# Two hybrid layers on one core: spectra and convolutions of the Hyena mixer in one stage, RWKV preparation in another order, output projection by pairs of tiles, first expert loaded during routing

## The reference

```python
def hier_moe(h, wg, bg, we, be, w_gate, w_up, w_down):      # 4 groups x 8 experts, top 2 in the best group
    ...
    hg = lax.ragged_dot(xs, w_gate, sizes); hu = lax.ragged_dot(xs, w_up, sizes)
    ys = lax.ragged_dot(jax.nn.silu(hg) * hu, w_down, sizes)
def hyena_mixer(u, ...):                                     # u: 1024 x 1536, three parts v, x1, x2
    h = hyena_filters(L, ...)                                # a small network's output @ w4, times a window
    z = x1 * long_conv(v, h[:, 0, 0], h[:, 0, 1], sk[0])     # both directions, by spectra of length 2048
    z = x2 * long_conv(z, h[:, 1, 0], h[:, 1, 1], sk[1])
def rwkv_mixer(u, ...):                                      # 8 heads of 64
    d = w0 + einsum('dblr,drc->dblc', tanh(wd), w2); decay = exp(-exp(-0.5) * sigmoid(d))
    a = sigmoid(a0 + einsum('dblr,drc->dblc', ad, a2)); g = sigmoid(gd) @ g2
    kk = heads(k * k_k); kk = kk / maximum(sqrt(sum(kk * kk, -1)), 1e-12)
    ...                                                      # the scan over tokens, both directions
    y = (y - mu_y) * rsqrt(var_y + RW_GN_EPS) * gn_w + gn_b  # per head
    y = (y + bonus) * g
def hybrid_layer(x, ...):
    x = layer_norm(DN_ALPHA * x + (g_h * y_h + g_r * y_r) @ w_o)
    ffn = (silu(x @ ffn_w_gate) * (x @ ffn_w_up)) @ ffn_w_down
    return layer_norm(DN_ALPHA * x + ffn)
```

## Time and profile before

| | |
|---|---|
| median of 3 runs | 4329.37 us (4329.35 to 4332.1) |
| profiled execution | 4336.35 us |
| its span | 4334.6 us |
| busy in it | PE 85%, DVE 66%, ACT 38%, POOL 1% |
| mean granted TensorE clock | 0.919 of full |
| bytes moved by DMA | 707.47 MB, mean 163 GB/s |

### The profile page before, as it was taken

The page is one execution under the profiler, slowest core; times in us unless marked ns, Lnnn a source line. Parts: engine busy times, 40 slices in busy tenths (PEclk is TensorE's granted clock), DMA queues, the critical chain, the costliest instruction groups (busy, mean ns, idle before and its releaser), DMA issues. The chain is left out here.

```text
span 4334.6 us, 62648 instructions
## 1 busy us (share of the span) xinstructions
PE 3668.8 (85%) x24897; PEld 2941.5 (68%) x24897; DVE 2840.1 (66%) x3459; ACT 1630.3 (38%) x2142; POOL 56.7 (1%) x50
## 2 busy tenths in 40 slices
PE   6999987979759999919999676439998786999897
PEld 4888876868747777717888232129996565888786
DVE  4775327966458888968875778765555547666455
ACT  3322114545247777733332110433332223333244
POOL 0000000000010000010000000000000000000000
PEclk8999999989779999959999788669999898999999
DMA  5933217545389999852332231471110432222455
GB/s 207 334 136 109 92 60 231 177 146 196 136 327 399 398 398 398 320 185 88 117 117 78 101 149 61 121 178 42 42 42 9 170 107 78 88 78 78 175 190 170
DMA packets 358292, 707.47 MB, mean 163 GB/s; under 512 B 55912, under 2 KB 160376, under 8 KB 355866
## 3 DMA queue, kind: packets, MB, share of 16 engines
q1 hardware_dynamic: 322698, 578.90, 38.7%
q10 hardware_dynamic: 20528, 67.11, 4.1%
q0 software_dynamic: 14816, 57.95, 3.7%
HBM read 536.18 MB, written 179.25 MB: 165 GB/s over the span
## 5 line engine op out<-in xcount | busy, mean ns | idle before, releaser
L1767 DVE TENSOR_TENSOR moe_wg_lo<-moe_wg,moe_wg_hi 128x2048 fp32r<-128x2048 f32 x68 | 155.7, 2292 | 68.9 <-ACT moe_wg_hi L1721 68.8
L156 PE MATMUL g_ps<-h1T_hi,g_w_lo 128*128 128x512 f32 x448 | 176.0, 393 | 6.9 <-DVE g_w_lo L355 6.9
L157 PE MATMUL g_ps<-h1T_lo,g_w_hi 128*128 128x512 f32 x448 | 175.5, 392 | 0.0
L158 PE MATMUL g_ps<-h1T_hi,g_w_hi 128*128 128x512 f32 x448 | 175.3, 391 | 0.0
L1721 ACT ACTIVATE moe_wg_hi<-moe_wg 128x2048 fp32r<-128x2048 f32 x68 | 130.3, 1920 | 95.5 <-DMA moe_wg<-in_exp_w_gate 95.5
L3929 DVE TENSOR_TENSOR x3T_lo<-fd_w_raw,x3T_hi 128x1024 fp32r<-128x1024 f32 x66 | 80.8, 1224 | 123.3 <-ACT x3T_hi L3858 123.1
L156 PE MATMUL g_ps<-x2T_hi,g_w_lo 128*128 128x512 f32 x352 | 140.0, 398 | 24.6 <-DVE g_w_lo L582 24.6
L2743 PE MATMUL rs_p_p<-rs_pm,rs_qx 64*64 64x64 f32 x2048 | 157.3, 217 | 0.0
L156 PE MATMUL fd_acc<-x3T_hi,x3T_lo 128*128 128x512 f32 x352 | 139.3, 396 | 20.0 <-DVE x3T_lo L3932 20.0
L1767 DVE TENSOR_TENSOR moe_wu_lo<-moe_wu,moe_wu_hi 128x2048 fp32r<-128x2048 f32 x68 | 152.6, 2285 | 2.3 <-ACT moe_wu_hi L1721 2.3
L156 PE MATMUL g_ps<-g_w_hi,h1T_lo 128*128 128x512 f32 x384 | 149.6, 390 | 0.0
(11 more groups left out here) (679 smaller groups left out, 10678.9 us busy)
## 6 DMA issues: line engine op xcount, KB each, us to landing
moe_wg<-in_exp_w_gate SPq DMA_DIRECT2D x68, 1024.0 KB
moe_wu<-in_exp_w_up SPq DMA_DIRECT2D x68, 1024.0 KB
moe_wd<-in_exp_w_down SPq DMA_DIRECT2D x66, 1024.0 KB
fd_w_raw<-in_ffn_w_down SPq DMA_DIRECT2D x66, 512.0 KB, 4.3
go_w_raw<-in_w_out SPq DMA_DIRECT2D x64, 512.0 KB
g_w<-in_w_in SPq DMA_DIRECT2D x52, 512.0 KB, 5.8
g_w<-in_w_in SPq DMA_DIRECT2D x22, 1024.0 KB
moe_x<-s_xs SPq DMA_DIRECT2D x34, 512.0 KB
```

The costliest lines, as they stand in the source:

```text
L156: pe.matmul(out, l[1], r[0], start=(k == 0), stop=False)
L157: pe.matmul(out, l[0], r[1], start=False, stop=False)
L158: return pe.matmul(out, l[0], r[0], start=False, stop=(k == kt - 1))
L1767: v.tensor_tensor(lo[:, q * m:q * m + m], w[:, q * m:q * m + m], hi[:, q * m:q * m + m], ALU.subtract).then_inc(sem_lo, 1)
```

## The change

Five pieces, in the order of the program:

1. **Routing** issues the loads of expert 0's three weight matrices (6.29 MB) behind its own loads, into raw buffers that now live outside both stages; `tile_exp` gets N_LIST more columns: whether a tile is used and has another expert than the tile before. **The expert loop** loads weights where that column says so, by two more register loads per tile; expert 0's loads are left out by the same condition.
2. **The two Hyena stages become one** (`hy`). The window is loaded before the transform table, v at the stage's start. PE turns v before the last transform and x1 after it, ACT alone copies both; DVE goes on from the last spectrum spread to the convolution's. The inverse table, x1 and the first spectrum planes are loaded during n = 3, into buffers that came free.
3. **RWKV preparation**: the low-rank inputs and weights are loaded first and decay, rate and gate of block 0 computed first; then the key's statistics, held as 128 x 256 (four column blocks at 32 rows each) instead of 32 x 1024, and spread through a zeroed 128 x 1024 tile (`spread_rows`). **RWKV finish** uses the constants that preparation left in its tiles, and the same 128 x 256 form.
4. **Output projection**: row tiles in the order 0, 4, 1, 5, 2, 6, 3, 7; the differences after each pair; the last sums as a group of three pairs (128 x 1536) and one of the last pair (128 x 512). It also loads the feed-forward's first gate weights (1 MB) during its norms.
5. **Feed-forward**: group 0 is there already, and its first unit is split before the four sums.

```diff
@@ route
+            for dst, src in first:
+                sp.dma_start(dst[:, :, :], rows(src)).then_inc(w_in, 16)
+            sp.wait_ge(w_in, past(16 * len(first)))
...
+            v.tensor_scalar(te[:, N_LIST + 1:N_LIST + 2], te[:, 0:1], 0.0, None, ALU.not_equal)
+            v.tensor_tensor(te[:, N_LIST + 2:], te[:, 1:N_LIST], te[:, 0:N_LIST - 1], ALU.not_equal)
+            v.tensor_copy(tile_exp[:, N_LIST:N_LIST + 1], te[:, N_LIST:N_LIST + 1])
+            v.drain()
+            v.tensor_scalar(tile_exp[:, N_LIST + 1:], te[:, N_LIST + 1:], te[:, N_LIST:N_LIST + 1], None, ALU.mult)
@@ experts
-                             cond=(n_used > j)).then_inc(sem[q], 16)
+                             cond=(limit > j)).then_inc(sem[q], 16)
...
-                e, e1 = expert(j), expert(j + 1)
+                e, e1, new, new1 = expert(j), expert(j + 1), fresh(j), fresh(j + 1)
@@ hyena, SP
-            sp.dma_start(tb[:, :, :], table).then_inc(table_in, 16)
             sp.dma_start(win[:, :, :], window).then_inc(win_in, 16)
-            for n in range(4):
+            sp.dma_start(tb[:, :, :], f_table).then_inc(table_in, 16)
+            sp.dma_start(raw[:, :, :], rows(conv[0:HY_W, :])).then_inc(v_in, 16)
...
+            for n in range(NF4):
+                if n == NF4 - 1:
+                    sp.wait_ge(turned, past(NT))
+                    sp.dma_start(raw[:, :, :], rows(conv[HY_W:2 * HY_W, :])).then_inc(x_in, 16)
+                    sp.wait_ge(windowed, past(16))
+                    sp.dma_start(it, i_table).then_inc(i_in, 16)
+                    sp.wait_ge(filt, past(16))
+                    for b in range(2):
+                        sp.wait_ge(spec_out[b], past(16 * (9 - b)))
+                    for i in range(NS):
+                        planes_in(0, i)
@@ hyena, PE
+                else:
+                    pe.wait_ge(v_in, past(16))
+                    pe.wait_ge(windowed, past(16))
+                    turn(z_act)
                 transform(n)
...
+            turn(x_act)
+            pe.wait_ge(taken, past(N_OUT))
+            pe.wait_ge(x_act, past(NT))
@@ rw_prepare and rw_finish
+def spread_rows(v, ri, riz):
+    for g in range(4):
+        r = slice(32 * g, 32 * g + 32)
+        e = v.tensor_copy(riz[r, g * RQ:g * RQ + RQ], ri[r, :])
...
+                        for g in range(4):
+                            mm = pe.matmul(p_r[:, 0:RQ], sel_s[:, q, 96 - 32 * g:224 - 32 * g], sq[:, q % 2, g * RQ:g * RQ + RQ],
+                                           start=(q == 0 and g == 0), stop=(q == RP - 1 and g == 3))
@@ product_norm
-                sp.dma_start(r[:, t % 2], x[t * P:t * P + P, :]).then_inc(x_in[t % 2], 16)
+                sp.dma_start(r[:, t % 2], x[ORDER[t] * P:ORDER[t] * P + P, :]).then_inc(x_in[t % 2], 16)
...
+            sp.dma_start(*early).then_inc(early_in, 16)
...
-                if t >= NT // 2:
-                    mix(t - NT // 2)
+                if t % 2:
+                    mix(t // 2)
...
+            low_sums(0, NP - 1, left_high, left_low)
+            low_sums(NP - 1, NP, mixed_high, mixed_low)
@@ ffn_up
-        w = [raw[:, 2 * b:2 * b + 2].rearrange("p a (k c) -> p (a k) c", c=256) for b in range(2)]
+        w = [w_first, raw[:, 2:4].rearrange("p a (k c) -> p (a k) c", c=256)]
...
+            split(0, 0)
             add_sums(0)
-            for i in range(7):
+            for i in range(1, 7):
                 split(0, i)
```

552 lines of the change are left out of this document (287 added, 265 removed).

## The result

| | before | after |
|---|---|---|
| median | 4329.56 us (4 runs, 4329.35 to 4332.1) | 4283.68 us (4 runs, 4277.1 to 4286.99) |
| profiled execution, its span | 4336.35, 4334.6 us | 4286.99, 4285.2 us |
| ratio | | 0.9892, 95% interval 0.9879 to 0.9904 |

The forecast was 4277 with a range of 4260 to 4296. The profiled executions differ by 49.4 us, the medians by 45.9. The times of the changed kernel scatter over 10 us, those of before over 3.

What follows compares the result with a forecast made beforehand. PE and DMA were taken to bound the expert loop, head-of-stage waits the other four places; 5 + 23 + 2 + 4 + 8.5 + 9.6 = 52 us off 4336.35 gave 4284, or 4277 for the median; range 4260 to 4296.

Steps and rivals of the forecast that it cites:

- Experts: Route and expert loop: preloading the first expert's weights brings its first products 5 us sooner; −5 us (0 to −10).
- the argument from bytes: Expert loop: 4.2 MB still to come at 1239.7, 10.5 us at 398 GB/s, is the most DMA can give.
- Hyena: Joint Hyena stage: −23 us (−18 to −27) from the join, −2 (0 to −4) from loading the window first.
- The slip: Hyena: 6.1 MB of loads ahead of the last eight spectrum stores delay the last transform's end from 2533.9 to near 2539.4.
- The window's order: Hyena's start: window loaded before the transform table, so the four window products are packed closer; −2 us (0 to −4).
- rw_prepare: RWKV preparation: reciprocal falls from 6.54 to 1.65 us, statistics move behind decay, rate and gate; −4 us (+4 to −6.5).
- The rival of the lower clock: PE stays at 1.2 GHz in the new stages: rw_prepare +8, rw_finish +2.5, hyena +3; 4291 us, chance 0.08.
- rw_finish: RWKV finish: no wait for constants, first matmuls at the upper clock, shorter reciprocal chain; −8.5 us (−6.5 to −11).
- Projection and feed-forward: Pairs end the projection's low sums sooner, first gate weights already loaded, first unit split first; −9.6 us (−8 to −11).
- Half of the join: Rival, Hyena: stores behind loads and ACT's copies hold PE back; −11 in place of −23, 4289 us, chance 0.11.
- the whole head start for the experts: Rival, expert loop: the weight stream, 10.5 us earlier, sets the end; 4271 us, chance 0.08.
- SP as a bound: Rival, expert loop: extra register loads and conditions make SP the bound, slower from 12.7 us per expert; chance 0.03.

Runs made afterwards that it cites:

- hy_late: Changed kernel, with the four spectrum planes, top plane and inverse table loaded behind the last eight spectrum stores: median 4280.65 us, Hyena stage 329.6 us.
- hy_only: Kernel before, with only its two Hyena stages replaced by the joint one: median 4309.74 us, ratio to before 0.9953.
- no_early: Changed kernel, with the feed-forward's first gate weights loaded at that stage's start again: median 4289.28 us, ratio to before 0.9904.

## Why the prediction was right, point by point

The forecast was 6.7 us below the measured median, well inside its range; the sum of 52 us stands against 45.9 by the medians.

- **Experts, −5 of 0 to −10: −6.5, in the mean of the profiles −5.5.** The size was right, the steps to it only in part. ACT's four halves without a gap came as forecast. The first load of expert 1 came 0.3 us sooner by the clock of the span, not 1.8 to 2.2; in the stage's own time the other nine profiles with the preload show 1.9 to 2.1 us, as forecast, but the stage opens 1.0 to 1.2 us later in all ten, where I had put 0.45 (the routing's first scatter is 0.43 us late, the rest is unexplained). Silu of the first expert, 1248.44, was 1.6 us sooner, not 5, and the last expert's silu stands 5.0 us nearer to the first's. The gain fits the argument from bytes: 6.3 MB less have to pass within the loop, and PE, whose own pace is 17.7 us and not 18.0 per expert, catches up in five to ten experts; then the weights bound it again. That the 5 us hit was luck in part: I had taken it from products that come 4 to 5 us sooner, and they came 1.6 us sooner.
- **Hyena, −25 of −18 to −31: −23.0, over nine profiles −23 to −30.** DVE's spread for the convolution stands 135.1 us after the stage's first load in place of 165.1, 30.0 sooner: 26.6 by the join, 1.1 by the first spread, and 2.3 by the transforms between, where PE had less of the lower clock (the first full one took 15.70 us in place of 17.00); 9.3 of it are lost again before PE's first inverse product (34.5 us behind the spread in place of 25.2), which leaves 20.7, in the forecast's 20 to 22.5; and 2.3 come behind it, 1.8 of them by the upper clock (3.60 us for what took 5.37). The slip was named rightly, as hy_late shows, and was larger where the lower clock came on top. The window's order: DVE's first product came 3.0 us sooner in the stage (+14.8 in place of +17.8), but the spread behind it only 1.1 us, since the filter matmuls are in its way; over all profiles with the new order that spread stands at +22.1 to +24.1, before at +23.3, so this part (−2) gave 1 us or nothing.
- **What was misread in the Hyena term.** The second input load of before landed 14.1 us after its issue, but the table was issued behind it, not ahead, so these are two loads of 2.1 MB in 14.5 us, some 290 GB/s, and not 398; the seven loads took 18.8 us in place of my 15.4. And the figures of this term are measured against one profile of before that was probably 7 us long in just these stages: by hy_only's median the join gives 20.6 us, 4 less than the forecast and within its range.
- **rw_prepare, −4 of +4 to −6.5: −0.1, over six profiles +0.8 to −3.8, −1.1 in the mean.** This is the term that was mis-sized. I put kk at 33 to 37 us after the first load; it came at 34.6 to 38.8. The failed step is "four squares with their matmuls to 2779 to 2780.6": in the stage's own time that was +28, and it was +30.6 (PE to 2753.77). From the root to the last copy 3.8 us passed, where I had 1.5 to 3.5, and the spread took 3.8 us, my upper value. In no_early, where the granted clock was 1.00 through the statistics, the same step ended at +28.1, as forecast, and the stage was 143.1 us, 3.8 below before: the chain was counted rightly for the upper clock, and the clock was the part put too low. The rival of the lower clock thus happened here by half (+3.9 of its +8), and in the Hyena stage of this profile with 3.0 us (10.15 and 15.60 against 8.80 and 13.97), its full +3; the difference of −23.0 hides that, since before had 4.1 us more of it elsewhere in the stage (the 2.3 and 1.8 us above). In rw_finish it did not happen.
- **rw_finish, −8.5 of −6.5 to −11: −9.0.** All three parts came: 3.0 us by PE's start without the wait for constants, and 6 us less from PE's start to the first scaled tile, of which 2.6 are the upper clock in the first eight matmuls.
- **Projection and feed-forward, −9.6 of −8 to −11: −8.7.** PE's first feed-forward matmul came 136.6 us after the projection's first load in place of 145.8, 9.2 us, as counted; 0.5 us were given back behind it, which I did not trace.
- **The rivals.** Half of the join, the whole head start for the experts, and SP as a bound did not happen. The slower case needed 12.7 us more per expert on SP; it was 1.2, and covered. The expert's step stayed at 18.4 to 18.5 us where the weights bound it.
- The sum was 52; the profiles differ by 49.4, of which 2.2 lie in stretches that the change does not touch.

## What to carry to other kernels

When loads are moved forward, look at what small stores stand behind them in the same queue and who waits for their buffers: here 4 MB placed eight stores too early took back 4 to 9 us of a gain of some 30. When a slow operation is made short, follow the chain from its input: a chain that is moved behind other work can use up the whole saving, and placing its short pieces into an engine's existing gaps gave 6 us in the mean without removing any work. And read a term's size from several profiles, of the kernel before too: the same code took up to 4.6 us more in one stage and up to 7.1 in another, and where the rows were compared, the granted clock differed.

## What the runs showed of the hardware that was not expected

A register load on SP with its part of the condition took 0.6 us in the loop, an estimate (32.6 us of waits gone for two in each of 27 tiles). The four passes of the spread took 3.78 us at the lower granted clock, 1.98 us at the upper one, and 2.61 or 3.00 where it changed in them, and in the same program they fell on either side from run to run: nine profiles of the same Hyena code span 7 us, six of the same rw_prepare 4.6 us. PE kept busy with unneeded matmuls held the upper clock, at 1.00 over 12 us, but in a chain of short waits that cost more than it gave. The two loads of 2.1 MB of the convolution's inputs moved at some 290 GB/s, where the weights of the experts moved at 398.
